# Expert stage of a streaming encoder step: blocks of 64 tokens in fixed order, four weight buffers, tokens stationary on column tiles

## The chip, the cores and the metric

The kernel runs on one NeuronCore of one Trainium2 chip; the other cores are idle. The metric is the device time of one launch in microseconds (us). Everything is float32. The engines that the text speaks of are TensorE (PE, with its weight loads, PEld), VectorE (DVE), ScalarE (ACT), GpSimd (POOL) and SyncE (SP); SP and POOL only matter here as queues that issue DMAs.

## The reference, cut to what matters

One layer over 512 prompt frames and 8 x 16 decode frames, 640 tokens of width 1024 in all: mixer (differential attention and a gated DeltaNet), cross-attention, then a hierarchical mixture of experts, then a last norm. The change touches only the mixture:

```python
grp_prob = softmax(x @ w_grp + b_grp);  g_top, g_idx = top_k(grp_prob, 1)     # 4 groups
e_logits = (x @ w_rt + b_rt).reshape(N, 4, 8)                                 # 8 experts in each
e_top, e_idx = top_k(e_logits of the chosen group, 2)
e_w = softmax(e_top) * g_top
out[n] = sum over the two chosen experts e of
         e_w * ( silu(x[n] @ w_gate[e]) * (x[n] @ w_up[e]) ) @ w_down[e]      # 1024 -> 256 -> 1024
```

So there are 1280 pairs of a token and an expert, spread unevenly over 32 experts, each with 3 MB of weights (gate, up and down 1 MB each), 96 MB together.

## The kernel before, in words

Everything up to the mixture is unchanged. The last cross-attention output jobs (`run_jobs` with "co", L415) alternate with the fourth norm ("ffn"). For each of the five token tiles POOL multiplies the normed row with the gain (L2015) and stores it to the DRAM tensor `h_rows` (L2017).

**Routing** (`route_pe`, `route_dve`). PE computes the logits (L1819, L1825), DVE finds group, first and second expert for every token by compares and reductions on 128 x 160 elements (the last of them L1907, `oh2`). A triangular matmul counts the pairs before each token (L1834, L1836). DVE derives blocks of CAP = 80 slots: each expert has as many blocks as it needs, in order of experts, so which expert a block belongs to is data (`table_u`), and so is the number of rounds of two blocks. A second group of matmuls (L1841) turns one-hot matrices into the table "slot to pair", from which come a column of token numbers and a column of pair numbers for every block.

**Expert stage** (`moe_sync`, `moe_pool`, `moe_pe`, `moe_act`, `moe_dve`). All five engines run a loop over rounds; a block j, with buffers of parity k, goes through these steps:

- SP reads the expert's number and loads gate, up (L2048) and down (L2051) into one of two weight buffers. Each load waits until PE has finished the matmuls of block j-2 that read the same part. `w_gate` and `w_up` go to SBUF so that partition p holds rows p, 128+p, ...: runs of 1 KB; `w_down` has runs of 4 KB.
- POOL gathers 80 rows of 4 KB of `h_rows` into `xg[k]` (indirect DMA, L2069), then waits for block j's result and scatters it to `pair_rows` (L2082). The order in its queue is: gather j+2, scatter j, gather j+3, scatter j+1, ...
- PE, in each block: gate and up (L2110: 32 matmuls, weights stationary, 80 tokens moving), the transposes of the next block's tokens (L2094, `turn(j+1)`), then down of the same block (L2119: 4 matmuls, hidden values stationary, 512 columns moving).
- ACT takes Silu of gate (L2135) and copies half of the transposes and of the result (L2128, L2139). DVE multiplies with up (L2164) and copies the other halves (L2151, L2169).

A float32 matmul appears in the trace as two instructions, each with its weight load; a transpose as one.

**End** (`final_*`). When all scatters have landed, POOL loads `pair_rows` back (L2194), DVE adds both rows of each token with their weights, norms, and SP stores the output (L2232).

Of the kernel before, what the change touches and what calls it, by code (L numbers as in the profile page):

```python
# [14 lines left out]
F32 = mybir.dt.float32  # L15
# [5 lines left out]
P = 128  # L21
D = 1024
KC = D // P
NT = 5
# [9 lines left out]
CAP = 80  # L34
MAXBLK = (NT * P * TOPK) // CAP + NE
BLKPAD = MAXBLK + 1
NBLK = BLKPAD + 5
NPAIR = TOPK * NT * P
EPS = 1e-6
# [8 lines left out]
def constant_columns():  # L48
# [23 lines left out]
    cols["capacities"] = np.repeat(CAP * np.arange(NT * P // CAP)[None] * 1.0, P, 0)  # L72
# [136 lines left out]
def build_encoder_step(nc, a):  # L209

    ctx = ExitStack()
    with ctx:
# [1571 lines left out]
        lgT = attn[0:36, 5504:5504 + NT * P]
        at_place = cmp_.rearrange("p a b -> p (a b)")[:, 0:2 * NT * CAP].rearrange("p (a b) -> p a b", b=CAP)
        assert at_r[0] <= 5120
        at_u = [5120]

        def us(n):
# [7 lines left out]
        e_pe = steps("moe_pe", "tr0 tr1 | gate up d0 d1")  # L1797
        r_pe = steps("route_pe", "lgp lgs lg cum table")
# [3 lines left out]
                      "dm w0 w1a w1 w2 A cnt pos capq nblk one ends "  # L1802
                      "cmp blk min tab cmp2 nr tabn starts base slotv s1a s1 s2a s2 off ib0 ib off2 place ap pairs "
# [18 lines left out]
        def route_pe(pe):  # L1822
# [17 lines left out]
            for i in range(2 * NT):  # L1840
                mm = nc.tensor.matmul(bank[2][0:CAP, 0:NBLK], at_place[:, i, :], in_block[:, i, :], start=i == 0, stop=i == 2 * NT - 1)  # L1841
# [686 lines left out]
```

## Time and profile before

| | us |
|---|---|
| three runs of the kernel | 1430.82, 1437.18, 1438.62; median 1437.18 |
| span of the profiled execution (first to last instruction) | 1429.8 |
| expert loads start on SP | about 999.5 |
| first gather issued on POOL | 1013.7 |
| first gate matmul on PE | 1020.2 |
| last copy of a result starts on DVE | 1392.3 |
| PE busy over the span | 1250.6 (87%) |

No separate time is given for the profiled execution: what is known of it is its span, 1429.8 us, and the median of the runs is 7.4 us above that. The expert stage is the last quarter of the span. On the page PE and the DMA engines both stand at 9 tenths in its slices; the "PEclk" row gives the granted TensorE clock, 1.0 being 2.4 GHz and 0.5 being 1.2 GHz.

### The profile page before, as it was taken

Reading aid. Unit: us, or ns where it says so; the run is one execution under the profiler, and the core shown is the slowest. Engines: PE = TensorE matmul, PEld = TensorE weight load, DVE = VectorE, ACT = ScalarE, POOL = GpSimd, SP = SyncE. Lnnn points to the kernel's source line nnn. Section 1 sums busy time; section 2 is a strip of 40 time slices with the busy share of each in tenths; the row PEclk is TensorE's granted clock in tenths of the full one; section 3 lists DMA queues with packets and bytes.
Section 4 is the critical chain, followed back from the end, with each engine's and each line's share of the span. In section 5 each row is a group of like instructions: output and inputs, shape, how many; then the busy total and the mean of one; then the engine's idle time right before and its main releaser. Section 6 shows DMA issues by size and latency. Waiting matters only on the chain.

```text
span 1429.8 us, 18302 instructions
## 1 busy us (share of the span) xinstructions
PE 1250.6 (87%) x7028; PEld 838.9 (59%) x7028; DVE 435.8 (30%) x949; ACT 310.1 (22%) x620; POOL 193.1 (14%) x222
## 2 busy tenths in 40 slices
PE   5999999987788789989999859994599999999990
PEld 3544555446677676654455644442577778777770
DVE  2002223326656564443210313345211111111115
ACT  2000557524223222102000212220011111111111
POOL 1000454301001001001000000031011111111114
PEclk9999999997989999999999979997599999999995
DMA  8111103111211314007460044410799999999966
GB/s 247 59 59 59 42 18 133 60 48 40 94 60 59 117 59 148 0 0 257 151 221 0 1 176 176 177 45 31 241 293 337 334 338 342 329 335 331 339 199 239
DMA packets 143148, 221.49 MB, mean 155 GB/s; under 512 B 18987, under 2 KB 93611, under 8 KB 142974
## 3 DMA queue, kind: packets, MB, share of 16 engines
q1 hardware_dynamic: 134564, 191.20, 40.1%
q0 software_dynamic: 8496, 29.50, 6.1%
q8 instruction: 31, 0.51, 0.1%
q10 hardware_dynamic: 42, 0.17, 0.1%
q14 instruction: 15, 0.12, 0.0%
HBM read 197.87 MB, written 22.97 MB: 154 GB/s over the span
## 4 chain that ended last, share of the span: by engine, by line
PE 72%; issue 15%; DVE 7%; DMA 2%; ACT 2%; POOL 1%; SPq 1%; DVEq 0%; POOLq 0%; ACTq 0%
PE bank L415 17%; PE bank L2110 16%; PE bank L411 14%; PE bank L2119 8%; PE bank L1074 3%; PE bank L2094 1%; PE bank L1614 1%; PE bank L1684 1%; DMA sb_W<-cache_mem_v 1%; PE bank L721 1%; PE bank L1079 1%; PE bank L741 1%; PE bank L357 1%; PE bank L1587 1%; PE bank L406 1%
## 5 line engine op out<-in xcount | busy, mean ns | idle before, releaser
L2110 PEld LDWEIGHTS bank<-sb_act_b,sb_W 128*128 128x128 f32 x2048 | 240.1, 196 | 17.2 <-issue 17.2
L2110 PE MATMUL bank<-sb_act_b,sb_W 128*128 128x80 f32 x2048 | 239.2, 279 | 0.9 <-DVE sb_act_b L2151 0.9
L415 PE MATMUL bank<-sb_W,sb_act_a 128*128 128x512 f32 x480 | 219.1, 603 | 1.7 <-issue 1.0
L411 PE MATMUL bank<-sb_act_a,sb_W 128*128 128x512 f32 (+1 forms) x768 | 213.1, 435 | 1.3 <-DVE sb_act_a L343 1.3
L411 PEld LDWEIGHTS bank<-sb_act_a,sb_W 128*128 128x128 f32 x768 | 116.0, 191 | 92.8 <-issue 90.7
L415 PEld LDWEIGHTS bank<-sb_W,sb_act_a 128*128 128x128 f32 x480 | 88.8, 193 | 101.2 <-issue 99.6
L2119 PE MATMUL bank<-sb_W,sb_act_b 128*80 128x512 f32 x256 | 118.8, 607 | 1.1
L1074 PE MATMUL bank<-sb_x 128*128 128x128 f32 x512 | 68.3, 284 | 9.7 <-DVE sb_x L1463 6.2
L2164 DVE TENSOR_TENSOR sb_act_b<-bank,sb_act_b 128x160 f32<-128x160 f32 x32 | 10.4, 324 | 216.3 <-PE bank L2110 216.3
L2119 PEld LDWEIGHTS bank<-sb_W,sb_act_b 128*80 128x80 f32 x256 | 36.4, 152 | 60.8 <-issue 60.8
L1074 PEld LDWEIGHTS bank<-sb_x 128*128 128x128 f32 x512 | 61.9, 194 | 16.3 <-DVE sb_x L1463 6.5
L2082 POOL DMA_INDIRECT pair_rows<-sb_act_b,sb_attn x32 | 29.6, 926 | 306.1 <-DVE sb_act_b L2169 306.1
L415 PE MATMUL bank<-sb_W 128*128 128x512 f32 x128 | 56.0, 593 | 1.4 <-DVE sb_W L343 1.4
L2169 DVE COPY sb_act_b<-bank 80x512 f32<-80x512 f32 x32 | 22.0, 687 | 100.2 <-PE bank L2119 100.2
L2128 ACT COPY sb_act_b<-bank 128x320 f32<-128x320 f32 x33 | 14.1, 426 | 147.9 <-PE bank L2094 147.9
L440 ACT COPY sb_conv<-bank 128x512 f32<-128x512 f32 x24 | 14.1, 586 | 147.8 <-PE bank L415 123.8
L321 POOL TENSOR_SCALAR sb_small<-sb_small 128x1 f32<-128x1 f32 x17 | 3.9, 232 | 298.7 <-ACT sb_scr L313 298.4
L415 PEld LDWEIGHTS bank<-sb_W 128*128 128x128 f32 x128 | 23.8, 190 | 29.4 <-issue 27.7
L415 PE MATMUL bank<-sb_conv,sb_act_a 128*128 128x512 f32 x80 | 39.4, 603 | 0.0
L2069 POOL DMA_INDIRECT sb_act_a<-h_rows,sb_attn x34 | 30.8, 907 | 57.0 <-DVE sb_attn L2147 47.3
L2135 ACT ACTIVATE sb_act_b<-bank 128x160 f32<-128x160 f32 x32 | 9.7, 304 | 129.6 <-PE bank L2110 129.6
L357 PE MATMUL bank<-sb_const,sb_scr 128*128 128x128 f32 x136 | 19.8, 303 | 19.5 <-DVE sb_scr L336 19.5
(381 smaller groups left out, 1487.9 us busy)
## 6 DMA issues: line engine op xcount, KB each, us to landing
sb_W<-w_gate SPq DMA_DIRECT2D x32, 1024.0 KB
sb_W<-w_up SPq DMA_DIRECT2D x32, 1024.0 KB
sb_W<-w_down SPq DMA_DIRECT2D x32, 1024.0 KB
sb_W<-w_in SPq DMA_DIRECT2D x7, 2048.0 KB, 8.3
sb_W<-cache_diff_k SPq DMA_DIRECT2D x8, 1024.0 KB, 5.2
sb_W<-cache_diff_v SPq DMA_DIRECT2D x8, 1024.0 KB, 7.4
sb_W<-cache_mem_k SPq DMA_DIRECT2D x8, 1024.0 KB, 4.8
sb_W<-cache_mem_v SPq DMA_DIRECT2D x8, 1024.0 KB, 7.0
```

The source lines that it names most:

```text
L357: mm = nc.tensor.transpose(quarters(bank[4 + 2 * (t % 2) + i])[:, c, :], scr[:, t % 2, q * P:(q + 1) * P], ident)
L406: mm = nc.tensor.matmul(out[0:8, 0:cols.stop - cols.start], w_gab[:, c, :], src[:, c, cols], start=c == 0, stop=c == KC - 1)
L411: mm = nc.tensor.matmul(out[:, 0:cols.stop - cols.start], slot(unit)[:, c, m * P:(m + 1) * P], src[:, c, cols], start=c == 0, stop=c == KC ...
L415: mm = nc.tensor.matmul(out[:, :], src[:, c, ja * P:(ja + 1) * P], w, start=c == 0, stop=c == KC - 1)
L721: mm = nc.tensor.matmul(bank[2 + m][:, 0:P * (t + 1)], dq[rows, h, t * P:(t + 1) * P], dk[rows, h, 0:P * (t + 1)], start=True, stop=True)
L741: mm = nc.tensor.matmul(bank[6 + t % 2][:, h * P:(h + 1) * P], aT[q][:, k * P:(k + 1) * P], dv[:, k, h * P:(h + 1) * P], start=k == 0, sto ...
L1074: mm = nc.tensor.matmul(quarters(out)[:, h, :], h4(lhs)[:, h, :], h4(rhs)[:, h, :], start=start, stop=stop)
L2069: pool.indirect_dma_start(xg[k][0:CAP, :], None, a["h_rows"], bass.IndirectOffsetOnAxis(token_col[k][0:CAP, :], 0))\
L2082: pool.indirect_dma_start(a["pair_rows"], bass.IndirectOffsetOnAxis(pair_col[k][0:CAP, :], 0), yb[k][0:CAP, :], None)\
L2110: mm = nc.tensor.matmul(bank[2 + m][:, CAP * f:CAP * f + CAP], w[:, c, f * P:(f + 1) * P], xgT[k][:, c, :], start=c == 0, stop=c == KC - 1)
L2119: mm = nc.tensor.matmul(bank[4 + g][0:CAP, :], hT[k][:, f, :], w[:, f, 512 * g:512 * g + 512], start=f == 0, stop=f == 1)
L2169: nc.vector.tensor_copy(yb[k][0:CAP, 512:1024], bank[5][0:CAP, :]).then_inc(e_dve.step("y1"), 1)
```

## The change

- CAP is 64. Blocks 0 to 31 are the first 64 pairs of experts 0 to 31, in this order, in code written out without a loop. Pairs beyond 64 of an expert go into overflow blocks behind them, in a loop over rounds of two blocks, at least one round.
- Tokens are the stationary operand: for each of 8 parts of the model width, two matmuls of 64 columns x 256 moving columns (128 of gate and 128 of up), the first half of the hidden width to PSUM partitions 0 to 63 (column tile 0), the second to 64 to 127 (column tile 1). Down is done likewise, 512 output columns on each tile.
- The hidden values come out with tokens on partitions, so one transpose per block (`turn_h`) and one more DVE copy are added; the copy of the result is one 128 x 512 copy on DVE, and ACT no longer takes part in it.
- A gathered block is 128 rows of 2 KB (two half rows per token), so there are 4 transposes of 128 x 128 in place of 8 of 80 x 128.
- PE's order in block j is now: gate and up of j, transposes of j+1, down of j-1, transpose of the hidden values of j.
- Weights of gate and up go to SBUF in runs of 8 KB; `h_rows` is written in a matching order of columns. There are four buffers (in `W`, `conv`, `act_a`, `gz`, `scr`), and the first three experts are loaded before the routing.
- The routing makes the table of the 32 first blocks directly behind the counts; the overflow table is computed afterwards, beside block 0.

The core of the diff:

```diff
-CAP = 80
+CAP = 64
+MAXMORE = NPAIR // CAP
+SLOTS = 4
...
         def moe_sync(sp):
...
+            def load(e, s, before):
...
+                for m, name in enumerate(("w_gate", "w_up")):
+                    if before is not None and m == 0:
+                        sp.wait_ge(e_pe["gu"], e_pe.after(before, "gu"))
+                    sp.dma_start(w_gu[s][:, m, :, :].rearrange("p c f -> p (c f)"),
+                                 of(name).rearrange("(p c) f -> p (c f)", c=KC)).then_inc(s_gu[s], 16)
+                if before is not None:
+                    sp.wait_ge(e_pe["d"], e_pe.after(before, "d"))
+                sp.dma_start(w_down[s], of("w_down").rearrange("(f p) d -> p f d", p=P)).then_inc(s_down[s], 16)
...
         def moe_pool(pool):
             for k in range(2):
+                pool.wait_ge(r_dve["token"], r_dve.after(0, "token"))
+                pool.indirect_dma_start(xg[k], None, a["h_rows"], bass.IndirectOffsetOnAxis(token_all[:, k:k + 1], 0)).then_inc(s_xg[k], 16)
+            for j in range(NE):
+                k = j % 2
+                pool.wait_ge(e_pe["tr"], e_pe.after(j, "tr"))
+                pool.indirect_dma_start(xg[k], None, a["h_rows"], bass.IndirectOffsetOnAxis(token_all[:, j + 2:j + 3], 0))\
                     .then_inc(s_xg[k], 16)
+                pool.wait_ge(e_dve["y"], e_dve.after(j, "y"))
+                pool.indirect_dma_start(a["pair_rows"], bass.IndirectOffsetOnAxis(pair_all[:, j:j + 1], 0), yb[k], None).then_inc(s_rows[k], 16)
...
         def moe_pe(pe):
+            def gate_up(j, k, s, count):
...
+                for c in range(KC):
+                    for f in range(2):
+                        mm = nc.tensor.matmul(bank[2 + k][CAP * f:CAP * f + CAP, 0:2 * P], xgT[k][:, c % 4, c // 4, :],
+                                              w_gu[s][:, :, c, f * P:(f + 1) * P], start=c == 0, stop=c == KC - 1, skip_group_check=True)
+                mm.then_inc(e_pe.step("gu"), 1)
+            def down(j, k, s, count):
...
+                for f in range(2):
+                    for g in range(2):
+                        mm = nc.tensor.matmul(bank[4 + k][CAP * g:CAP * g + CAP, :], hT[k][:, CAP * f:CAP * f + CAP],
+                                              w_down[s][:, f, 512 * g:512 * g + 512], start=f == 0, stop=f == 1, skip_group_check=True)
             turn(0, 0, 16)
+            for j in range(NE):
+                gate_up(j, j % 2, j % SLOTS, 32 * (j // SLOTS + 1))
+                turn(j + 1, (j + 1) % 2, 16 * ((j + 1) // 2 + 1))
+                if j:
+                    down(j - 1, (j - 1) % 2, (j - 1) % SLOTS, 16 * ((j - 1) // SLOTS + 1))
+                turn_h(j, j % 2)
+                if j == 0:
+                    route_more_pe(pe)
```

PE, one block of the loop before. L2110 is gate and up, L2094 the transposes of the next block, L2119 down:

```order
L2110 MATMUL bank<-sb_act_b,sb_W 128x80 x32
L2090 ISA
L2094 MATMUL bank<-sb_const,sb_act_a 128x80 x8
L2114 ISA
L2117 ISA
L2119 MATMUL bank<-sb_W,sb_act_b 80x512 x2
L2117 REGISTER_ALU
L2119 MATMUL bank<-sb_W,sb_act_b 80x512 x2
```

PE, two blocks of the changed kernel. L2156 is gate and up, L2147 the transposes of the next block, L2171 down of the previous block, L2163 the transpose of the hidden values:

```order
L2156 MATMUL bank<-sb_conv,sb_act_b 64x256 x16
L2147 MATMUL bank<-sb_const,sb_act_a 128x128 x4
L2171 MATMUL bank<-sb_W,sb_act_b 64x512 x4
L2163 MATMUL bank<-sb_const,sb_act_b 128x128
L2156 MATMUL bank<-sb_act_a,sb_act_b 64x256 x16
L2147 MATMUL bank<-sb_const,sb_act_a 128x128 x4
L2171 MATMUL bank<-sb_gz,sb_act_b 64x512 x4
L2163 MATMUL bank<-sb_const,sb_act_b 128x128
```

Down has moved from the block whose gate and up stand before it to the next one: between gate and up of block j and its down there are now gate and up of j+1 and the transposes of j+2.

POOL in the loop before (one round of two blocks); L2069 is the gather, L2082 the scatter:

```order
L2067 REGISTER_ALU
L2069 DMA sb_act_a<-h_rows,sb_attn 80x1024
L2080 ISA
L2082 DMA pair_rows<-sb_act_b,sb_attn 1440x1024
L2066 ISA
L2067 REGISTER_ALU
L2069 DMA sb_act_a<-h_rows,sb_attn 80x1024
L2080 ISA
L2082 DMA pair_rows<-sb_act_b,sb_attn 1440x1024
```

POOL in the changed kernel, the first gathers and blocks; L2117 and L2123 are gathers, L2128 is the scatter:

```order
L2117 DMA sb_act_a<-h_rows,sb_attn 128x512 x2
L2123 DMA sb_act_a<-h_rows,sb_attn 128x512
L2128 DMA pair_rows<-sb_act_b,sb_attn 2816x512
L2123 DMA sb_act_a<-h_rows,sb_attn 128x512
L2128 DMA pair_rows<-sb_act_b,sb_attn 2816x512
```

The order of gathers and scatters in POOL's queue has not moved (gather j+2, scatter j); the register instructions between them are gone in the first 32 blocks.

## Rows read from the trace of the kernel before

**Rows 1.** Windows: after the length, busy us of PE, PEld, DVE, ACT, POOL; then clock, DMA share, GB/s.
```profile
1100.00:1150.00 50.00, 49.86 (x366) 40.47 (x366) 6.64 (x21) 8.12 (x15) 8.20 (x9) 1.00 1.04 336
```

**Rows 2.** Timeline of one block: start, us, engine, line, what, idle before.
```profile
1202.14 0.90 POOL L2069 DMA_INDIRECT sb_act_a<-h_rows,sb_attn  x1 [0.30 <-issue]
1206.30 0.72 PE L2094 MATMUL bank<-sb_const,sb_act_a 80*128 80x80 f32 x8
1207.04 3.65 PE L2119 MATMUL bank<-sb_W,sb_act_b 128*80 128x512 f32 x8
...
1210.54 7.27 PE L2110 MATMUL bank<-sb_act_b,sb_W 128*128 128x80 f32 x64
...
1210.74 0.69 DVE L2169 COPY sb_act_b<-bank 80x512 f32<-80x512 f32 x1 [3.07 <-PE bank L2119]
1212.25 0.93 POOL L2082 DMA_INDIRECT pair_rows<-sb_act_b,sb_attn  x1 [9.20 <-DVE sb_act_b L2169]
1213.48 0.90 POOL L2069 DMA_INDIRECT sb_act_a<-h_rows,sb_attn  x1 [0.30 <-issue]
1214.41 0.38 SPq L2048 DMA_DIRECT2D sb_W<-w_gate  x1
1217.53 0.67 PEld L2094 LDWEIGHTS bank<-sb_const,sb_act_a 80*128 80x128 f32 x8
1217.83 0.37 SPq L2048 DMA_DIRECT2D sb_W<-w_up  x1
```

**Rows 3.** Waits of SP's queue, 1060 to 1400 us: total, times, longest.
```profile
SPq L2048 <- PE bank L2110: 136.2, 54, 2.9
SPq L2051 <- PE bank L2119: 104.2, 28, 3.7
```

**Rows 4.** All gathers (L2069), from issue until landed.
```profile
DMA to landing us min/median/max: 4.1/6.9/9.1
```

**Rows 5.** Windows with the DMA engines full: 1 KB runs, then 4 KB runs.
```profile
1022.00:1026.00 4.00, 4.00 (x21) 4.00 (x20) 0.00 (x0) 0.00 (x0) 0.00 (x0) 0.50 1.13 357
1408.00:1414.00 6.00, 0.00 (x0) 0.00 (x0) 5.38 (x6) 2.30 (x4) 2.77 (x4) 0.50 1.02 414
```

**Rows 6.** Timeline: transposes (L1684), four column tiles (L1691), full-array matmuls (L415).
```profile
866.56 1.04 PE L1684 MATMUL bank<-sb_const,sb_W 128*128 128x128 f32 x8
870.13 1.07 PE L1691 MATMUL bank<-sb_attn 128*32 128x256 f32 x16
871.12 0.30 PEld L415 LDWEIGHTS bank<-sb_W,sb_act_a 128*128 128x128 f32 x2 [0.41 <-issue]
946.18 7.03 PE L415 MATMUL bank<-sb_W,sb_act_a 128*128 128x512 f32 x16
```

**Rows 7.** Windows around a pause of PE, before, in and behind it.
```profile
637.40:642.80 5.40, 0.00 (x0) 0.00 (x0) 4.12 (x7) 0.00 (x0) 1.01 (x1) 0.69 0.00 0
642.80:649.60 6.80, 6.08 (x10) 2.90 (x11) 2.30 (x3) 2.78 (x5) 1.71 (x4) 0.50 0.57 207
649.60:656.00 6.40, 6.40 (x16) 2.85 (x15) 4.61 (x5) 4.61 (x8) 3.86 (x8) 1.00 0.57 206
```

**Rows 8.** Timeline from the routing to the first block.
```profile
987.21 0.33 DVE L1907 TENSOR_TENSOR sb_attn<-sb_const,sb_attn 128x160 f32<-128x160 f32 x1
990.09 2.29 PE L1836 MATMUL bank<-sb_attn,sb_const 128*128 128x160 f32 x10
1004.78 0.99 DVE L1978 TENSOR_TENSOR sb_attn<-sb_const,sb_attn 128x800 f32<-128x800 f32 x1
1006.46 2.92 PE L1841 MATMUL bank<-sb_attn 128*80 128x54 f32 x20 [14.09 <-DVE sb_attn L1980]
1013.69 1.00 POOL L2069 DMA_INDIRECT sb_act_a<-h_rows,sb_attn  x1 [42.50 <-DVE sb_attn L2147]
1020.16 13.94 PE L2110 MATMUL bank<-sb_act_b,sb_W 128*128 128x80 f32 x64 [0.88 <-DVE sb_act_b L2151]
```

**Rows 9.** A POOL queue step in straight code (h_rows store), and the last result copy.
```profile
970.59 0.60 POOL L2017 DMA_DIRECT2D h_rows<-sb_conv  x1 [0.30 <-POOL sb_conv L2015]
1392.34 0.69 DVE L2169 COPY sb_act_b<-bank 80x512 f32<-80x512 f32 x1 [3.07 <-PE bank L2119]
```

More of the change, by code:

```diff
@@ L1796, in build_encoder_step @@
         token_col, pair_col = [us(1), us(1)], [us(1), us(1)]
-        e_pe = steps("moe_pe", "tr0 tr1 | gate up d0 d1")
-        r_pe = steps("route_pe", "lgp lgs lg cum table")
+        e_pe = steps("moe_pe", "tr | gu | ht | d")
+        r_pe = steps("route_pe", "lgp lgs lg cum first more")
         r_act = steps("route_act", "lgp lgs ge ee")
@@ L1801, in build_encoder_step @@
                       "A0 lg gmax gs ge4 gsum gtop gq gq2 gidx msk0 msk1 ml m1 d1 q1 q1b i1 oh1 ml2 m2 d2 q2 q2b i2 oh2 "
-                      "dm w0 w1a w1 w2 A cnt pos capq nblk one ends "
-                      "cmp blk min tab cmp2 nr tabn starts base slotv s1a s1 s2a s2 off ib0 ib off2 place ap pairs "
-                      "e0 e1 pf pu p1 p2 p3 p4 token")
+                      "A fi dm w0 w1a w1 w2 cnt dsel sel ap token e0 pf pair "
+                      "capq nmore one ends cmp more min tab cmp2 nr tabn starts base do osel low os slot off im0 im off2 place "
+                      "mi token2 e2 pf2 pair2")
         s_route = sem("route_weights_loaded")
@@ new lines, in route_dve @@
+            ts(token_all[:, 0:NE], table[:, 1, :], 2.0, C("half"), ALU.mult, ALU.add).then_inc(r_dve.step("token"), 1)
+            n0, n1 = slice(0, NE), slice(NE, NBLK)
+            stt(over_f[:, n0], table[:, 0, :], 0.0, C("empty")[:, n0], ALU.is_equal, ALU.mult).then_inc(r_dve.step("e0"), 1)
+            dve.wait_ge(r_dve["e0"], r_dve.after(0, "e0"))
+            stt(pair_f[:, n0], table[:, 0, :], -1.0, over_f[:, n0], ALU.add, ALU.add).then_inc(r_dve.step("pf"), 1)
+            dve.wait_ge(r_dve["pf"], r_dve.after(0, "pf"))
@@ L1967, in route_dve @@
-            tt(off, sl12.unsqueeze(2).to_broadcast([P, 2 * NT, NBLK]), C("slot0").unsqueeze(1).to_broadcast([P, 2 * NT, NBLK]),
+            for k in range(2):
+                ins = tt(dd_all[:, k, :, :], oh_all[:, k, :, :], row(starts, NE), ALU.mult)
+            ins.then_inc(r_dve.step("do"), 1)
+            dve.wait_ge(r_dve["do"], r_dve.after(0, "do"))
+            red(osel, dsum, AX.X, ALU.add).then_inc(r_dve.step("osel"), 1)
+            ts(low, sel, float(CAP), -1.0e6, ALU.is_le, ALU.mult).then_inc(r_dve.step("low"), 1)
@@ new lines, in result @@
+            def result(j, k, count, table=None):
+                dve.wait_ge(s_rows[k], count)
+                if table is not None:
+                    nc.vector.tensor_copy(pair_col[k], table).then_inc(e_dve.step("pc"), 1)
+                dve.wait_ge(e_pe["d"], e_pe.after(j, "d"))
+                nc.vector.tensor_copy(yb[k], bank[4 + k][:, :]).then_inc(e_dve.step("y"), 1)
+            for j in range(NE):
+                hidden(j, j % 2)
+                if j:
+                    result(j - 1, (j - 1) % 2, H_ROWS[(j - 1) % 2] + 16 * ((j - 1) // 2))
+                hidden_turned(j, j % 2)
+                if j == 0:
+                    route_more_dve(dve)
```

408 lines of the change are left out of this document (214 added, 194 removed).

## The prediction, as put on record before the changed kernel ran

> **What bounds the kernel now.** I read the 40 slices of the page first: from slice 29 on PE and the DMA engines both stand at 9. Which of them is the limit is not told by shares, so I took the windows [rows 1]: in 50 us of the expert stage PE is busy 49.86 us, at the full clock, and the DMA engines also count as full (share 1.04) at 336 GB/s. Then the timeline of one block [rows 2]: gate and up 7.27 us, transposes 0.72, down 3.65 (the rest is overlap); the scatter starts at 1212.25, the gather of the same block at 1213.48 and the gather before at 1202.14, so a block takes 1213.48 - 1202.14 = 11.34 us. PE's parts fill it. The waits of SP's queue [rows 3] show who waits: weight loads wait for PE (54 and 28 times), and in the block's rows PE waits neither for weights nor for a gather. So PE sets 11.34 us, 32 blocks in 16 rounds: 363 us. The DMA engines are close behind: a block moves 3.15 MB of weights, 0.33 MB gathered and 0.33 MB scattered, 3.80 MB; at the 357 GB/s of the stretch with runs of 1 KB alone [rows 5] that is 10.7 us.
>
> **The change part by part.** The number of blocks: the router applied to the reference's inputs gives two experts with more than 64 pairs (70 and 71) and none empty, so there are 32 + 2 = 34 blocks, one overflow round.
>
> PE's own work per block. Sixteen instructions of 512 columns on the full array take 7.03 us, 439 ns each [rows 6], so one of 256 columns would take 220 ns. On four column tiles 16 instructions of 256 columns took 1.07 us where 16 x 220 = 3.5 us would stand in a row: 3.3 of 4 tiles overlap [rows 6]. I take the same share on two tiles, 1.65. Gate and up: 32 instructions x 220 / 1.65 = 4.3 us. Down: 8 x 439 / 1.65 = 2.1 us. Transposes: 4 + 1 at 130 ns (eight in 1.04 us, [rows 6]) = 0.65 us. There is up to 0.41 us of idle where PE goes from column tiles back to the full array [rows 6]; four such changes of mode per block, 0.2 each, are 0.8 us. Sum 7.9 us, against 11.34: 3.4 us less. If the tiles did not overlap it would be 7.0 + 3.5 + 0.65 + 0.8 = 12 us.
>
> The Trainium skill (TensorEngine Tiling (Array Packing), Key Properties) says that a change of tiling mode drains TensorE. It gives no price; the 0.41 us of idle behind L1691 is the nearest row, and with it in full at all four places PE's sum would be 8.7 us.
>
> DMA. Down's 4 KB runs were there before; gate's and up's become 8 KB. A stretch with 4 KB runs only moved 414 GB/s with a share of 1.02 [rows 5]. A block moves 3.15 + 0.26 + 0.26 = 3.67 MB: 8.9 us at that rate. So PE and the DMA engines would both allow about 9 us a block.
>
> The chain that I think decides instead. POOL's queue keeps its order, gather j+2, scatter j; the gather of j+3 stands behind the scatter of j, which waits for the copy of block j's result. Before, that gather's block is needed by the transposes one block after the copy, and down of j+2, whose result frees the queue again, stands behind them: the circle copy, scatter, gather, transposes, down, copy covers two blocks, 22.7 us, and there it is never late. Now down of j+1 stands right behind the transposes of j+3: y(j), scatter(j), gather(j+3), transposes(j+3), down(j+1), y(j+1). This circle covers one block. What it costs, from the end of down to the end of the next down:
> - copy of the result on DVE: 0.1 + 0.69 = 0.8 us [rows 2].
> - until POOL issues the scatter: 1212.25 - 1211.43 = 0.82 before, with register work; 0.30 in straight code [rows 9]. I take 0.3.
> - issue of the scatter 0.93, 0.30 to the gather [rows 2]: 1.2 us. It has 128 rows where it had 80; if the issue grows with the rows it is 1.5 + 0.3.
> - gather from issue to landed: 6.9 us median, 4.1 to 9.1 [rows 4]. The low end is a gather with empty DMA queues. Now it meets the fullest moment: SP's load of down for block e waits for down of e-4, and gate and up of e+1 then wait for nothing, so 3 MB (7.6 us at 414 GB/s) are queued at every end of a down, 2 to 3 us ahead of the gather. I take 7.0 us, and 9.1 as the upper end.
> - transposes 0.1 + 0.5, change of mode 0.2: 0.8 us.
> - down 2.1 us.
> Sum 0.8 + 0.3 + 1.2 + 7.0 + 0.8 + 2.1 = 12.2 us at the full clock.
>
> The Trainium skill (DMA: Bandwidth & Descriptors, Queues, rings and completion order) says that each DMA engine takes its queues in turn, a packet from one and then from the next. A packet of weights would be 8 KB where it is 1 KB now, so each of the gather's and scatter's 16 packets per engine would wait for one of these. At 414/16 = 26 GB/s an engine needs 0.32 us for 8 KB and 0.08 for 2 KB, so the pair would take 16 x 0.40 = 6.4 us from its first packet on; that points to 8 or 9 us of landing, and a period of 13.5 us at the full clock. That is the upper half of my range, not its middle.
>
> The clock. PE works turn_h and gate and up (4.7 us) while the gather is under way, which lands 9.3 us after down's end: it stands still for 4 to 5 us in every block. A pause of 5.4 us in the trace took the clock from 1.0 to 0.5, and it stayed there for 6.8 us of work [rows 7]. So transposes and down, which are on the circle, run mostly at 1.2 GHz: 0.5 + 2.1 us more when all of it does. Then gate and up is slower too, the pause gets shorter, and in some blocks the clock is back. I take a third of it, 0.8 us: period 13.0 us. Bounds: 12.2 (never low) and 14.8 (always).
>
> The start. The counts' matmuls follow `oh2` (987.54, [rows 8]) at once: 991. Selecting, reducing and the 128 x 1280 one-hot (0.99 x 1280/800 = 1.6 us, [rows 8]): 994.3. Twenty instructions of 128 stationary columns, by L1841's 2.92 us for 80 columns: 4.4 us, then tokens and POOL: gather at 999.3, landed 4.1 later, PE's first gate at about 1005, where it was 1020.2. So 15 us earlier. Gate and up of block 0 at the low clock 8.6 us, overflow table 4.4, gate and up of block 1, transposes, then the first down ends at about 1026. The routing for the overflow (some 25 DVE operations of 0.2 to 1.6 us, 11 us) lies beside block 0.
>
> The end. The last copy of a result starts 1392.34, the span ends 37.5 us later [rows 9]; nothing in it changes but POOL's gather waits: 38 us. The last three blocks have no weights beside them: 2.5 us less each.
>
> Sum: 1026 + 33 x 13.0 - 7 + 38 = 1486 us of span. The runs' median is 7.4 us above the profiled span of 1429.8, so 1493 us.
>
> **Rivals.**
> 1. The gather is not late, or its landing is short (4 to 5 us, as with empty queues), since weights now come in fewer, longer runs. Then the circle is 0.8 + 0.3 + 1.2 + 4.1 + 0.8 + 2.1 = 9.3 us, just above the DMA engines' 8.9, PE pauses too little to lose the clock: 1026 + 33 x 9.3 + 38 = 1371, 1378 us as a run. For it: the 4.1 us exist, and the queue of indirect DMAs is another one than SP's. Against it: a median of 6.9 under less load than there will be. It decides if a gather lands in under 5.1 us at the full clock (11.1 us is the period at which old and new are equal: (1430 - 1026 - 38) / 33).
> 2. The column tiles overlap little or not. Down is 3.5 us and the circle 13.6 at the full clock, 12 us of PE work are no longer hidden well, the period is 14.7: 1026 + 485 + 38 - 7 = 1542, 1549 us. Against it: 1.07 us for sixteen instructions.
> 3. The landing is about 6 us and the clock holds: period 11.1, no change, 1437. It needs two things to meet.
> 4. The gather's packets each wait for a long one: landing 8.3 us, and the low clock in a third of the blocks, period 12.2 + 1.3 + 0.8 = 14.3: 1026 + 472 - 7 + 38 = 1529, 1536 us. For it: 8 KB runs in the queue at that moment. Against it: among 1 KB and 4 KB runs the landing was never over 9.1 [rows 4]. (This is what the Trainium skill's rule above would make of the time; the trace neither bears it out nor excludes it.)
>
> **How the numbers follow.** About 0.5% is what a measurement of this kernel can tell from no change. My forecast with rivals 2 and 4, all slower: 0.45, 0.07 and 0.12. Rival 1, with what lies between it and rival 3: 0.30. Rival 3: 0.06. Predicted 1493. The forecast's own range is 1455 (period 12.0) to 1535 (14.3). The range that holds 8 in 10 goes down to 1385, a period of 9.5, and up to 1545.
>
> **What would show it.** In the changed profile the transposes (L2147) should wait for the gather's landing in nearly every block, with 3 to 5 us each, and not L2156 for weights; the scatter L2128 should wait for the copy L2238, and gathers take 7 us or more to land. The clock should alternate between 0.5 and 1.0. Gate and up in 4.3 us says the tiles overlap, 7 that they do not. First gate at 1005. If PE waits for nothing there, or for weights at over 400 GB/s, the circle is wrong and the time lies near 1378.

## The result, and the profile after

The changed kernel is slower: 1537.91 us median of 4 runs (1535.41 to 1541.69) against 1434.24 us of the kernel before (4 runs on the same chip, 1430.82 to 1438.62). The ratio is 1.0725, with a 95% interval of 1.0701 to 1.0748. The forecast was 1493 us in a range of 1385 to 1545. The profiled execution took 1541.69 us, 1539.9 of it span (1.8 us less than the time of the same run), at a mean granted clock of 0.869.

The windows of the expert stage are the place to begin, as in [rows 1] (length, busy us of PE, PEld, DVE, ACT, POOL, then clock, DMA share, GB/s):

```profile
1110.00:1160.00 50.00, 25.36 (x141) 11.61 (x136) 3.83 (x10) 2.87 (x7) 5.87 (x6) 0.74 0.68 264
1210.00:1260.00 50.00, 30.50 (x168) 13.93 (x166) 4.43 (x11) 2.59 (x6) 7.40 (x8) 0.74 0.61 230
```

PE, busy 49.86 us of 50 before, is busy for half of the time; the DMA engines fell from 336 GB/s to 230 to 264. Neither is the bound any longer: something makes both wait. The waits between 1060 and 1490 us name it (total, times, longest):

```profile
POOL pair_rows L2128 <- DVE sb_act_b L2238: 371.5, 30, 14.7
...
PE bank L2147 <- DMA sb_act_a<-h_rows,sb_attn: 176.3, 29, 8.4
```

In 29 blocks the transposes (L2147) wait for the gathered rows, 6.1 us each on average, and POOL in its turn waits for the copy of a result. The timeline of one block shows the two in a circle (it answers to [rows 2]; start, us, engine, line, what, idle before and its releaser):

```profile
1226.83 0.33 PE L2163 MATMUL bank<-sb_const,sb_act_b 128*128 128x128 f32 x1
1226.94 0.38 SPq L2096 DMA_DIRECT2D sb_W<-w_down  x1
1227.02 0.69 DVE L2238 COPY sb_act_b<-bank 128x512 f32<-128x512 f32 x1 [10.14 <-PE bank L2171]
...
1227.09 3.67 PE L2156 MATMUL bank<-sb_act_a,sb_act_b 128*64 128x256 f32 x32
1227.36 0.47 SPq L2092 DMA_DIRECT2D sb_conv<-w_gate  x1
...
1227.88 0.43 SPq L2092 DMA_DIRECT2D sb_conv<-w_up  x1
1227.99 0.99 POOL L2128 DMA_INDIRECT pair_rows<-sb_act_b,sb_attn  x1 [12.29 <-DVE sb_act_b L2238]
1229.28 0.97 POOL L2123 DMA_INDIRECT sb_act_a<-h_rows,sb_attn  x1 [0.30 <-issue]
...
1237.41 1.12 PE L2147 MATMUL bank<-sb_const,sb_act_a 128*128 128x128 f32 x4 [6.65 <-DMA sb_act_a<-h_rows,sb_attn]
...
1238.46 3.69 PE L2171 MATMUL bank<-sb_gz,sb_act_b 128*64 128x512 f32 x8
...
1242.26 0.69 DVE L2238 COPY sb_act_b<-bank 128x512 f32<-128x512 f32 x1 [10.85 <-PE bank L2171]
```

From copy to copy: 0.97 us until POOL issues the scatter, 1.29 to the issue of the gather, 8.13 until the transposes begin, 1.05 to down, 3.80 to the next copy. The sum is 15.24 us. The SP rows show what goes into the queues just ahead of the gather: three loads of 1 MB, 1.4 to 2.3 us before it. Windows around this gather and the one before (same columns as above) show the two resources largely taking turns:

```profile
1216.00:1222.50 6.50, 0.23 (x4) 0.00 (x0) 0.29 (x1) 0.28 (x1) 0.00 (x0) 0.74 1.03 425
1223.00:1226.50 3.50, 3.50 (x12) 1.41 (x12) 0.00 (x0) 0.58 (x1) 0.00 (x0) 0.57 0.01 2
1226.50:1230.80 4.30, 4.26 (x35) 2.36 (x33) 0.89 (x2) 0.00 (x0) 1.96 (x2) 1.00 0.59 202
1230.80:1237.40 6.60, 0.00 (x0) 0.00 (x0) 0.29 (x1) 0.28 (x1) 0.00 (x0) 0.65 1.03 417
1237.40:1244.00 6.60, 6.59 (x25) 2.70 (x27) 0.89 (x2) 0.58 (x1) 0.77 (x1) 0.57 0.15 19
```

For some 6.5 us of each block the DMA engines run at 417 to 425 GB/s and PE stands still; during the transposes and down they move next to nothing (2 GB/s). Only beside gate and up do both work (the third row, 202 GB/s). That is why both look half idle. The last column but two is the clock, 1.0 being full speed: during transposes and down, behind the pause, it is 0.57, mostly the low level, and during gate and up it is back at 1.00.

The 30 gathers of L2123 between 1040 and 1500 us, and three copies of results (first block, block 27, last):

```profile
DMA to landing us min/median/max: 3.5/8.0/9.8
```

```profile
1031.50 0.69 DVE L2238 COPY sb_act_b<-bank 128x512 f32<-128x512 f32 x1 [1.86 <-PE bank L2171]
...
1438.12 0.69 DVE L2238 COPY sb_act_b<-bank 128x512 f32<-128x512 f32 x1 [10.12 <-PE bank L2171]
...
1502.71 0.69 DVE L2238 COPY sb_act_b<-bank 128x512 f32<-128x512 f32 x1 [3.84 <-PE bank L2171]
```

The period of the steady part is (1438.12 - 1031.50) / 27 = 15.06 us, where the kernel before has (1346.94 - 1040.49) / 27 = 11.35. Below, "period" is this same quotient, from the copies of blocks 0 and 27 of each kernel, unless another stretch is named.

### The profile page after: what moved, and what is told of

It is laid out like the page before. It is cut to its first block, busy times and chain, and to the rows that moved or that the text cites. A ratio compares the mean times of both kernels' runs of the same rounds, so it can differ in the third digit from the quotient of the medians.

```text
span 1539.9 us, 15256 instructions
## 1 busy us (share of the span) xinstructions
PE 1177.8 (76%) x6014; PEld 682.7 (44%) x6014; DVE 429.3 (28%) x900; ACT 278.1 (18%) x577; POOL 209.5 (14%) x226
## 4 chain that ended last, share of the span: by engine, by line
PE 52%; issue 17%; DMA 17%; DVE 7%; POOL 4%; ACT 2%; SPq 1%; DVEq 0%; POOLq 0%; ACTq 0%
DMA sb_act_a<-h_rows,sb_attn 15%; PE bank L416 15%; PE bank L412 13%; PE bank L2171 7%; PE bank L1075 2%; PE bank L2147 2%; POOL pair_rows L2128 2%; DVE sb_act_b L2238 1%; PE bank L1615 1%; PE bank L1685 1%; DMA sb_W<-cache_mem_v 1%; PE bank L722 1%; DVE sb_scr L337 1%; PE bank L1080 1%; PE bank L742 1%
## 5 line engine op out<-in xcount | busy, mean ns | idle before, releaser
L2147 PE MATMUL bank<-sb_const,sb_act_a 128*128 128x128 f32 x140 | 37.2, 417 | 198.3 <-DMA sb_act_a<-h_rows,sb_attn 198.3
L2147 PEld LDWEIGHTS bank<-sb_const,sb_act_a 128*128 128x128 f32 x140 | 23.8, 208 | 213.8 <-DMA sb_act_a<-h_rows,sb_attn 204.2
L2238 DVE COPY sb_act_b<-bank 128x512 f32<-128x512 f32 x34 | 23.5, 692 | 324.6 <-PE bank L2171 324.6
L2128 POOL DMA_INDIRECT pair_rows<-sb_act_b,sb_attn x32 | 31.6, 988 | 402.9 <-DVE sb_act_b L2238 402.9
L2156 PE MATMUL bank<-sb_W,sb_act_b 128*64 128x256 f32 x512 | 63.5, 404 | 3.6 <-issue 3.6
L2202 ACT COPY sb_act_b<-bank 128x512 f32<-128x512 f32 x35 | 20.5, 585 | 234.8 <-PE bank L2147 234.8
L2171 PE MATMUL bank<-sb_W,sb_act_b 128*64 128x512 f32 x128 | 52.4, 966 | 0.0
L2207 ACT ACTIVATE sb_act_b<-bank 128x128 f32<-128x128 f32 x34 | 9.4, 277 | 228.6 <-PE bank L2156 228.6
L2156 PEld LDWEIGHTS bank<-sb_W,sb_act_b 128*64 128x64 f32 x512 | 37.8, 147 | 24.8 <-issue 8.8
L2226 DVE TENSOR_TENSOR sb_act_b<-bank,sb_act_b 128x128 f32<-128x128 f32 x34 | 9.9, 292 | 116.7 <-ACT sb_act_b L2207 116.7
```

The costliest lines, as they stand in the source:

```text
L2128: pool.indirect_dma_start(a["pair_rows"], bass.IndirectOffsetOnAxis(pair_all[:, j:j + 1], 0), yb[k], None).then_inc(s_rows[k], 16)
L2147: mm = nc.tensor.transpose(quarters(bank[k])[:, c, :], xg[k][:, c * P:(c + 1) * P], ident)
L2156: mm = nc.tensor.matmul(bank[2 + k][CAP * f:CAP * f + CAP, 0:2 * P], xgT[k][:, c % 4, c // 4, :], w_gu[s][:, :, c, f * P:(f + 1) * P], sta ...
L2171: mm = nc.tensor.matmul(bank[4 + k][CAP * g:CAP * g + CAP, :], hT[k][:, CAP * f:CAP * f + CAP], w_down[s][:, f, 512 * g:512 * g + 512], st ...
L2202: nc.scalar.copy(xgT[k].rearrange("p i h s -> p (i h s)"), bank[k][:, :]).then_inc(e_act.step("xt"), 1)
L2238: nc.vector.tensor_copy(yb[k], bank[4 + k][:, :]).then_inc(e_dve.step("y"), 1)
```

## Experiments

Each experiment edits the changed kernel, unless another one is named. Times are medians of the runs. Periods, landings and windows are read from one profiled execution of each kernel; landings are medians of the gathers between 1060 and 1300 us.

**1. Undo the circle on GpSimd.** Only the order of POOL's queue is changed: the scatter is one block late.

```diff
             for j in range(NE):
                 pool.wait_ge(e_pe["tr"], e_pe.after(j, "tr"))
                 pool.indirect_dma_start(xg[k], ... token_all[:, j + 2:j + 3] ...)
-                pool.wait_ge(e_dve["y"], e_dve.after(j, "y"))
-                pool.indirect_dma_start(a["pair_rows"], ... pair_all[:, j:j + 1] ..., yb[k], None)
+                if j:
+                    scatter(j - 1)
+            scatter(NE - 1)
```

> GpSimd's static order is shifted: gather of block j+2, then the scatter of block j-1, whose result is already on its way, where the changed kernel has gather j+2, scatter j. Nothing else is changed. Theory (the circle covers one block: copy, scatter issue, gather issue, landing 8.0 us, transposes, down): the circle now spans two blocks, so a block costs at most half of 15.1 us, and the next bound is DMA at 8.9 us or PE at 7.9 us; with frictions 9.5 us a block, 28 blocks by 5.6 us less, 1380 us. Rival 1 (the weights' loads set the period, since SP waits 383.6 us in this stage and each load waits for a down): 1530 to 1545 us, PE's waits move from the gather to the weights. Rival 2 (PE at the low clock sets it, gate and up 6.3 us plus down 3.7 us plus transposes 1.1 us and mode changes): 12 to 13 us a block, 1450 to 1480 us, granted clock still alternating.

Measured: 1346.97 us (1343.56 to 1348.20), ratio to the kernel before 0.9382 [0.9356, 0.9407]. That is 191 us less than the changed kernel, by moving one instruction in a queue, and below the forecast of the theory. The windows, and PE's waits between 1060 and 1300 us (group: busy, mean ns, then idle before and releaser):

```profile
1110.00:1160.00 50.00, 40.86 (x265) 23.44 (x261) 6.77 (x17) 5.17 (x12) 10.79 (x12) 0.93 1.02 416
```

```profile
L2160 PE MATMUL bank<-sb_W,sb_act_b 128*64 128x256 f32 x384 | 52.4, 434 | 22.8 <-DMA sb_W<-w_up 22.8
...
L2151 PE MATMUL bank<-sb_const,sb_act_a 128*128 128x128 f32 x108 | 17.7, 287 | 1.0 <-DMA sb_act_a<-h_rows,sb_attn 1.0
```

The wait for gathers is gone (1.0 us), though a gather still takes 7.6 us to land. PE now waits for weights (22.8 us in this group, 46.0 over all buffers), at 416 GB/s. Once the buffers that were filled early are used up, blocks 9 to 27 come every 8.89 us, close to DMA's own price (3.67 MB at 416 GB/s are 8.82 us).

**2. Undo the circle on TensorE instead.** GpSimd's order stays the changed kernel's; down of a block goes back into that block, and VectorE's copies of results follow.

```diff
                 turn(j + 1, (j + 1) % 2, 16 * ((j + 1) // 2 + 1))
-                if j:
-                    down(j - 1, ...)
                 turn_h(j, j % 2)
                 if j == 0:
                     route_more_pe(pe)
+                down(j, j % 2, j % SLOTS, 16 * (j // SLOTS + 1))
```

> Only the place of the down projection is changed: TensorE does gate and up of block j, transposes of j+1, hidden's transpose and down of block j, instead of down of block j-1; VectorE's order follows. GpSimd's order is the changed kernel's (gather j+2, scatter j). Theory of the circle: down(j) no longer stands behind the transposes of a block whose gather waits for the scatter before it; the circle spans two blocks, and a block costs PE's own 7.9 us plus two waits of PE on the chain gate, SiLU, product, transpose, copy (some 1.5 to 2.5 us): 10 to 11 us, 1400 to 1430 us. Rival 1 (loads set the period): 1530 us or more. Rival 2 (the low clock sets it): 13 to 14 us a block, 1480 to 1510 us.

Measured: 1337.70 us (1337.38 to 1339.02), ratio 0.9328 [0.9306, 0.9349]. The forecast of the theory was 1400 to 1430. The one-block circle can thus be broken at either end. My price for PE's waits was too high; one block in its timeline:

```profile
1184.72 3.67 PE L2156 MATMUL bank<-sb_W,sb_act_b 128*64 128x256 f32 x32 [1.78 <-DMA sb_W<-w_up]
...
1188.32 0.66 PE L2147 MATMUL bank<-sb_const,sb_act_a 128*128 128x128 f32 x4
...
1189.09 0.33 PE L2163 MATMUL bank<-sb_const,sb_act_b 128*128 128x128 f32 x1
...
1189.80 1.94 PE L2171 MATMUL bank<-sb_W,sb_act_b 128*64 128x512 f32 x8 [0.39 <-DVE sb_act_b L2229]
...
1193.54 3.67 PE L2156 MATMUL bank<-sb_conv,sb_act_b 128*64 128x256 f32 x32 [1.80 <-DMA sb_conv<-w_up]
```

The transposes of the next block hide gate and SiLU; only 0.39 us remain in front of down. While weights lie ready the first blocks come every 6.8 us; then DMA sets 8.88 us (blocks 12 to 27). The clock is 0.97 to 1.00 here, the DMA engines move 416 GB/s in each window of 50 us, and PE still waits 1.8 us a block for weights: the stage is bound by DMA.

**3. The same circle without weights.** Loads only for experts 0 to 3 (and for the overflow); the other blocks use what lies in the four buffers, so the output is not the reference's.

```diff
-                load(e, e % SLOTS, e - SLOTS if e >= SLOTS else None)
+                if e < SLOTS:
+                    load(e, e % SLOTS, None)
```

> The weights of experts 4 to 31 are not loaded (every block uses what lies in the four buffers), so the output is not the reference's; the orders and all waits of GpSimd, ACT and DVE are the changed kernel's. Theory (landing is long because the gather's packets stand among the weights' packets): the gather lands in 3.4 to 4.1 us as with empty queues, not 8.0, and the circle of one block falls from 15.1 to some 11 us, less if the clock holds: 1400 to 1420 us, PE still waits for the gather in every block. Rival (the landing is the gather's own, whatever else is in the queues): 8.0 us stay and the time stays at 1530 us or more.

Measured: 1384.02 us (2 runs, 1382.73 to 1385.32), below the 1400 to 1420 of the theory; period 9.47 us.

```profile
1204.38 0.97 POOL L2124 DMA_INDIRECT sb_act_a<-h_rows,sb_attn  x1 [0.30 <-issue]
...
1207.74 0.66 PE L2148 MATMUL bank<-sb_const,sb_act_a 128*128 128x128 f32 x4 [1.88 <-DMA sb_act_a<-h_rows,sb_attn]
```

```profile
DMA to landing us min/median/max: 3.3/3.4/3.7
```

The landing falls from 8.0 to 3.4 us with the spread gone, so the other 4.6 us are the weights' traffic. PE still waits for the gather in every block. The period fell by 5.6 us. The 1.0 us beyond the landing fits the clock, since PE pauses less: blocks in which down runs at the full level (1.94 us) come every 8.2 to 8.4 us, those in which it takes 3.1 to 3.6 us every 9.5 to 10.6, where the changed kernel has down at 2.9 to 3.7 us.

**4. Runs of 1 KB, natural rows.**

```diff
-                    nc.gpsimd.tensor_tensor(h_row[...].rearrange("q (c p) -> q c p", c=KC), by_chunk(scr[...]), by_chunk(gffn_row), ALU.mult)
+                    nc.gpsimd.tensor_tensor(h_row[:, t % 2, :], scr[:, t % 2, :], gffn_row, ALU.mult)
-                                 of(name).rearrange("(p c) f -> p (c f)", c=KC))
+                                 of(name).rearrange("(c p) f -> p c f", c=KC))
```

> Gate and up weights are read in runs of 1 KB (row c*128+p on partition p) as the kernel before did, and h_rows are written in their natural order, so that GpSimd's product of the norm is contiguous again. Everything else is the changed kernel's. Theory (long packets lengthen the landing, 8.0 against 6.9 us): landing back to 6.9 us, one us less in each of 28 blocks, and 6 to 8 us earlier routing: 1495 to 1505 us; the loads take 10.3 us a block instead of 8.9, still below the period. Rival 1 (the length of the runs has no part in the landing): 1530 us, by the start alone. Rival 2 (eight times as many packets in the queues ahead of the gather make it land later): above 1545 us.

Measured: 1519.45 us (1514.91 to 1524.21), ratio 1.0587 [1.0548, 1.0625]; landing 7.7 us, period 14.55. Eight times as many packets, each an eighth as long, do not delay the gather; it lands 0.3 to 0.4 us earlier (8.1 us is the changed kernel's median in the same stretch, 8.0 in the longer one). This is a net figure, since packets of 1 KB also move more slowly (experiment 9). The expectation of the theory was 15 to 25 us too low: the landing was to fall by 1.1 us, and the routing was to come 6 to 8 us earlier, where the first copy of a result came 2.4 us earlier (1029.11). The length of the runs has a small part in the landing.

**5. Fill PE's pause.**

```diff
                 gate_up(j, j % 2, j % SLOTS, 32 * (j // SLOTS + 1))
+                if j > 2:
+                    for _ in range(22):
+                        nc.tensor.matmul(bank[7][:, 0:P], ident, ident, start=True, stop=True)
                 turn(j + 1, ...)
```

> The changed kernel, with 22 multiplications of the identity by itself (128 x 128, some 0.22 us each at the full clock, into bank 7) on TensorE between gate and up of block j and the transposes of block j+1, from block 3 on; they lie in the 6.7 us in which TensorE waits for the gather. Theory (the low clock adds to the circle, since down took 2.9 to 3.7 us and the transposes up to 1.1 us): with the pause filled the clock holds, down falls to 2.0 us and the transposes to 0.7 us, and a block costs 1.5 to 2 us less, 13.1 to 13.6 us: 1480 to 1495 us. Rival 1 (the clock stays low whatever fills the pause, and the filler then takes 9.4 us and holds the transposes up): 1560 us or more. Rival 2 (the clock rises and the time stays, since other steps of the circle set it): 1530 to 1540 us.

Measured: 1518.48 us (1511.82 to 1519.38), ratio 1.0589 [1.0559, 1.0618], period 13.93; landing 8.3.

```profile
1110.00:1160.00 50.00, 42.05 (x324) 29.89 (x325) 4.42 (x11) 3.17 (x7) 6.71 (x7) 1.00 0.68 263
```

```profile
1228.84 0.66 PE L2147 MATMUL bank<-sb_const,sb_act_a 128*128 128x128 f32 x4 [2.98 <-DMA sb_act_a<-h_rows,sb_attn]
...
1229.43 1.94 PE L2171 MATMUL bank<-sb_gz,sb_act_b 128*64 128x512 f32 x8
```

Work that computes nothing makes the kernel 19 us faster: the granted clock is 1.00 in this window where it was 0.74, transposes and down take 0.66 and 1.94 us. The periods of the two profiled executions differ by 1.1 us, but the one of this kernel was its fastest run (1511.82) and that of the changed kernel its slowest (1541.69); the medians give 19.4 / 28 = 0.7 us a block. So the clock had a price of at least 0.7 us a block. It is less than I expected (1.5 to 2, and 1480 to 1495 us), since down still took 3.58 us in some blocks, and landing rose a little:

```profile
1213.30 3.58 PE L2171 MATMUL bank<-sb_W,sb_act_b 128*64 128x512 f32 x8
```

**6. One load, behind the gather.** Experts from 4 on load w_gate only, and up and down use what lies in the buffers, so here too the output is not the reference's. The load waits for gate and up, not for a down.

```diff
-                for m, name in enumerate(("w_gate", "w_up")):
+                for m, name in enumerate(("w_gate", "w_up") if whole else ("w_gate",)):
...
+                if not whole:
+                    return
                 if before is not None:
                     sp.wait_ge(e_pe["d"], e_pe.after(before, "d"))
```

> The changed kernel's orders, with only w_gate loaded for the experts from 4 on (1 MB a block instead of 3; up and down use what lies in the buffers, so the output is not the reference's). It places the gather's landing between 3.4 us without weights and 8.1 us with three loads. Theory (the gather's packets share the DMA engines with all weight packets that the same down's end released, so the landing grows with the bytes in the queues): one load of 2.4 us beside it, landing 5 to 6 us, period 11 to 12 us, 1430 to 1450 us. Rival (each gather packet waits for at most one long packet, whatever stands behind it): landing as with three loads, 7.5 us or more, 1520 us or more.

Measured: 1378.58 us (2 runs, 1378.34 to 1378.81), landing 3.4 us, period 9.57. Both expectations missed; the timeline says why: the load is issued after the gather.

```profile
1216.74 0.97 POOL L2125 DMA_INDIRECT sb_act_a<-h_rows,sb_attn  x1 [0.30 <-issue]
1218.48 0.33 SPq L2092 DMA_DIRECT2D sb_W<-w_gate  x1
...
1220.27 0.66 PE L2149 MATMUL bank<-sb_const,sb_act_a 128*128 128x128 f32 x4 [1.83 <-DMA sb_act_a<-h_rows,sb_attn]
```

As a test of bytes it decides nothing. It does show that 1 MB issued 1.7 us after the gather (0.8 us after the end of its 0.97 us of issue) does not hold it up: the landings are 3.3 to 3.9 us.

**7. The same three loads, earlier in the circle.** They wait in addition for the next transposes, so they come 3.9 to 5.9 us ahead of a gather's issue, not 1.4 to 2.3.

```diff
                     sp.wait_ge(e_pe["d"], e_pe.after(before, "d"))
+                    if isinstance(e, int):
+                        sp.wait_ge(e_pe["tr"], e_pe.after(e - 1, "tr"))
```

> The changed kernel with one more wait on the queue engine (SP): the burst of three loads that it issues when a down has ended now waits also for the next transposes, so for the landing of a gather. The burst begins some 5.5 us before the next gather is issued, not 1.3 us before it; all loads, their bytes and the orders of the other engines are the changed kernel's. Theory (a gather lands late by the weight bytes that are still ahead of it in the queues): at 414 GB/s the 3 MB take 7.6 us, so some 2 us of them are left, and the gather lands in 5 to 6 us instead of 8.1; period 12.5 to 13 us, 1455 to 1480 us. Rival 1 (a gather beside any full-rate stream takes 8 us, wherever the stream began): no change, 1530 to 1540 us. Rival 2 (the loads come too late for their block and PE waits for weights): above 1540 us.

Measured: 1482.15 us (1476.36 to 1483.72), ratio 1.0321 [1.0281, 1.0360]; period 12.91. Landing and period are as the theory has them, the time is 2 us above its 1455 to 1480. First and last load of one burst, the gather behind it, and all landings:

```profile
1221.36 0.38 SPq L2098 DMA_DIRECT2D sb_gz<-w_down  x1
...
1223.09 0.48 SPq L2092 DMA_DIRECT2D sb_act_a<-w_up  x1
...
1227.28 0.97 POOL L2125 DMA_INDIRECT sb_act_a<-h_rows,sb_attn  x1 [0.30 <-issue]
```

```profile
DMA to landing us min/median/max: 5.3/6.0/8.2
```

Holding loads back gives 56 us: an added wait makes the kernel faster. It follows that the overlap in time of the burst with the gather is what lengthens the landing. It does not follow that a gather stands behind all bytes that were queued ahead of it. In experiments 1 and 2 the queues are never empty, and a load of w_up lands some 26 us after its issue, but the gather in 7.6 and 7.5 us. Two rows of experiment 2 (KB each, median us to landing):

```profile
sb_W<-w_up SPq DMA_DIRECT2D x10, 1024.0 KB, 26.4
...
sb_act_a<-h_rows,sb_attn POOLq DMA_INDIRECT x28, 7.5
```

It shares the engines with the loads and lands ahead of most of them.

**8. Down in its block, natural rows, two runs of 4 KB.** Experiment 2 with the contiguous product, gate and up rows h*512 + 4p + c on partition p, and transposes that read every fourth element:

```diff
-                                 of(name).rearrange("(p c) f -> p (c f)", c=KC))
+                                 of(name).rearrange("(h p c) f -> p h (c f)", h=2, c=4))
-                    mm = nc.tensor.transpose(quarters(bank[k])[:, c, :], xg[k][:, c * P:(c + 1) * P], ident)
+                    mm = nc.tensor.transpose(quarters(bank[k])[:, c, :], xg[k].rearrange("q (p c) -> q c p", c=4)[:, c, :], ident)
```

> The kernel with down in its own block, in which in addition h_rows are written in their natural order (GpSimd's product of the norm is contiguous) and gate and up weights come in two runs of 4 KB to a partition, row h*512 + 4p + c on partition p; the transposes of the gathered rows read every fourth element. Theory (GpSimd's strided product delays the routing by 6 to 8 us, and runs of 4 KB move as fast as runs of 8 KB): 1337.7 less 6 to 8, 1329 to 1333 us, DMA at 414 to 416 GB/s in the stage. Rival 1 (4 KB runs are slower in the full queues, 5%): 270 us of loads become 284, 1345 us. Rival 2 (the strided reads slow the transposes): no change of the period as long as PE stays below 8.8 us a block; only the start shows.

Measured: 1336.55 us (5 runs, 1333.09 to 1342.36), ratio 0.9331 [0.9303, 0.9358]: no different from experiment 2. The start is earlier as forecast (first copy of a result at 1017.92, not 1025.59, so 7.7 us), but the DMA engines move 409 to 410 GB/s where 416 stood, and blocks 12 to 27 take 9.02 us, not 8.88. The time lies between the theory (1329 to 1333) and its rival of slower 4 KB runs (1345). A bound by DMA does not care that the first block starts sooner, beyond the loads that this lets go earlier.

**9. The same with runs of 1 KB.** Experiment 2 with the edit of experiment 4.

> The kernel with down in its own block, with gate and up weights in runs of 1 KB and h_rows in natural order. In this kernel the loads bound the block, so the run length must show. Theory: at 357 GB/s (the rate of the kernel before with 1 KB runs) the 3.67 MB of a block take 10.3 us instead of 8.8, 28 blocks by 1.5 us more, less 6 to 8 us for the routing: 1370 to 1378 us. Rival (the DMA engines work 1 KB packets off as fast when the queues are full): 1330 us.

Measured: 1363.79 us (1358.92 to 1366.21), ratio 0.9507 [0.9474, 0.9540].

```profile
1110.00:1160.00 50.00, 35.34 (x239) 20.21 (x237) 6.37 (x15) 4.32 (x10) 10.65 (x11) 0.97 1.07 373
```

Between the theory and the rival. Full queues move 1 KB runs at 373 GB/s, more than the 357 of [rows 5] and less than 416. Blocks 12 to 27 take 9.79 us. Here the long runs earn their keep, 26 us, which the circle had hidden in experiment 4, where the short ones were faster.

In the table the landings are those named above; the kernel before has the median of all its gathers [rows 4].

| kernel | median us | gather lands, us | period us |
|---|---|---|---|
| changed | 1537.9 | 8.0 | 15.06 |
| 4: 1 KB runs | 1519.5 | 7.7 | 14.55 |
| 5: filler | 1518.5 | 8.3 | 13.93 |
| 7: loads earlier in the circle | 1482.2 | 6.0 | 12.91 |
| before | about 1435 | 6.9 | 11.35 |
| 3: no weights | 1384.0 | 3.4 | 9.47 |
| 6: one load, behind the gather | 1378.6 | 3.4 | 9.57 |
| 9: experiment 2 with 1 KB runs | 1363.8 | 6.4 | 9.79 (blocks 12 to 27) |
| 1: scatter one block late | 1347.0 | 7.6 | 8.89 (blocks 9 to 27) |
| 2: down in its block | 1337.7 | 7.5 | 8.88 (blocks 12 to 27) |
| 8: experiment 2 with 4 KB runs | 1336.6 | 7.0 | 9.02 (blocks 12 to 27) |

## Why the prediction was right, and where it was off

**The circle.** Right, and shown: the landing of the gather is waited for in 29 blocks (6.65 us in the block above), and breaking the circle at either end takes 191 and 200 us off with the same bytes and the same matmuls. I had put a kernel without it near 1378; it does 1338 to 1347. The wait was twice as long as I wrote (6.1 us a block, not 3 to 5).

**PE's own work.** Close, and somewhat too high: 3.67 us for gate and up where 4.3 was forecast (32 x 0.22 = 7.0 in a row, so 1.9 of 2 tiles overlap, not 1.65), 1.94 for down (2.1), 0.66 and 0.33 for the transposes. The parts add up to 6.6 us, and in experiment 2 with ready weights a block is 6.8 us; I had 7.9. Rival 2 is out. The changes of mode cost almost nothing: in the changed kernel's block, L2163 (full array) and L2156 (column tiles) follow the work ahead within 0.1 us, where I had 0.2 to 0.4.

**DMA.** 8.9 us a block at 414 GB/s was forecast, 8.88 at 416 is what experiment 2 runs at.

**The landing.** 7.0 us in the sum, 8.0 measured. The text named the cause (3 MB queued 2 to 3 us ahead of the gather, 1.4 to 2.3 in the trace) and then took nearly the old median [rows 4]. Experiments 3 and 7 give the sizes: 3.4 us alone, 6.0 with the burst partly over, 8.0 in the midst of it. Mis-sized by 1.0 to 1.1 us a block.

**The clock.** 0.8 us for a third of the blocks. In the block above both the transposes (1.12) and down (3.80 to the copy) run at the low level; against 0.59 and 2.05 of experiment 5 that is 2.2 us (1.05 + 3.80 - 0.59 - 2.05), in place of 0.8. Some blocks do better (down was 2.93 us in the one before). The mean clock of the stretch was 0.74, but what counts is its level while transposes and down run, 0.57 in the windows above, and the term should have been near its upper bound. How much of the 2.2 us the full clock gives back on average is not shown: the filler of experiment 5 gave 0.7 to 1.1 us, with some blocks still slow.

**The period.** 13.0 forecast, bounds 12.2 to 14.8, 15.06 measured: above the upper bound. In the block shown, 15.24 = 12.2 + 1.1 (landing) + 2.2 (clock against the full level as measured) - 0.3 (the small steps and down's overlap, measured a little shorter).

**Rival 4.** It gave 14.3 us and 1536 us, and this time is nearer than the forecast's. That is luck, since its mechanism is not what made it: with 1 KB packets in place of 8 KB the landing fell by 0.3 to 0.4 us, not by the 1.3 us between its 8.3 and my 7.0. The Trainium skill (DMA: Bandwidth & Descriptors, Queues, rings and completion order) says that an engine takes its queues in turn, one packet each. The direction agrees in the kernels with full queues, where the median landing was 6.4 us beside 1 KB, 7.0 beside 4 KB and 7.5 beside 8 KB packets (experiments 9, 8, 2); the size does not. My estimate from it, 8 x (0.31 - 0.04) = 2.2 us for the gather's eight packets on each engine at the trace's 26 GB/s, is twice the 1.1 us seen. The estimate takes one run of the loads for one packet of the rule, as the prediction did; that section of the Trainium skill counts some 9 to 17 descriptors in a packet, so what fails here is my reading, and the rule as it stands is not tested.

**The start.** Missed by 11 us: first gate at 1015.84, forecast 1005. I put the permuted product on GpSimd at nothing, as if it took as long as before. The groups of this line (five tiles, before 1010 us) in the kernel before, then in the changed one:

```profile
L2015 POOL TENSOR_TENSOR sb_conv<-sb_scr,sb_conv 128x1024 f32<-128x1024 f32 x5 | 12.2, 2437 | 11.5 <-DVE sb_scr L336 11.4
```

```profile
L2053 POOL TENSOR_TENSOR sb_conv<-sb_scr,sb_conv 128x1024 f32<-128x1024 f32 x5 | 19.6, 3922 | 12.8 <-DVE sb_scr L337 11.4 <-DMA h_rows<-sb_conv 1.4
```

Its strided operands make it 2.44 to 3.92 us, 7.4 us over the five tiles, and the routing stands behind it. The router's first VectorE operation on the logits comes at 987.83 in the changed kernel and at 986.07 in experiment 2, where the kernel before has 979.66; with the contiguous product it comes at 979.20 in experiment 8. Experiments 9 and 4 have that product too and stand at 981.87 and 985.40, so the sign is shown and the size varies from run to run. Another 2.4 us lie behind the first gather: from its issue (1007.70) to the first gate are 8.1 us, where I had 5.7; PE is idle for 3.56 us just ahead of the gate, and why is open. The copy of the first block came only 5.5 us late (1031.5 for 1026): gate and up of block 0 took 6.30 us, mostly at the low clock, where 8.6 stood, and the matmuls of the overflow table 2.33 us at the full clock, where 4.4 stood.

**The sum.** 1031.5 + 471.2 (34 copies, the last blocks shorter) + 37.2 to the end = 1539.9 us of span. Forecast: 1026 + 422 + 38 = 1486. 49 of the 54 us lie between the first and the last copy (27 periods that were 2.06 us longer, 55.6 in all, less 6.4 since the last six steps took 64.6 us where 71 was in the sum), 5.5 are the start's, the tail gives 0.8 back. The last step of the sum was wrong too: I added 7.4 us to get from span to time, the distance of the median from the span of one execution. Where both are known for the same run, the time is 1.8 to 2.0 us above the span, so the sum stands for 1488 us, and the 5.6 us too many brought it nearer to the result by luck.

The sign and the mechanism were right; the time was 3% low, and 3 us outside the forecast's own range (1455 to 1535). Both uncertain terms were set too low, the landing at 7.0 us of 4.1 to 9.1 and the clock at 0.8 of 0 to 2.6, and they add.

## What to carry to other kernels

Count over how many iterations each circle of waits runs, through every in-order queue in it. Moving down behind the transposes put one more engine's order into a circle that already held GpSimd's; it went from two blocks to one, and a latency of 7 to 8 us that had been free became more than half of the period. Where a latency cannot be shortened, issue the operation that waits for late data behind the one that others wait for: here the scatter behind the next gather, worth 191 us.

When two terms of a circle are uncertain, ask what they do to each other: here a longer landing meant a longer pause, and the low clock came with it (down took 2.9 to 3.7 us at 8.0 us of landing, 1.94 to 3.6 at 3.4), so both belonged at the same end of their ranges.

## What was not expected of the hardware

- A gather of 128 rows lands in 3.4 us (3.3 to 3.7) with empty queues, about 8 us in the midst of a burst of 3 MB, and 7.5 us with queues that are never empty, where a load of 1 MB lands some 26 us after its issue. So it neither stands behind all that was queued before nor goes first.
- Dummy matmuls in a pause made the kernel 19 us faster, though the transposes and down on the circle are only some 3 us a block at the full clock.
- Full queues moved 416 GB/s with 8 KB runs of gate and up, 410 with 4 KB and 373 with 1 KB (down's 4 KB runs, gathers and scatters among them).
- Two column tiles of 64 overlapped almost in full in fp32: 32 instructions of 256 columns in 3.67 us, 115 ns each.
